# Stick-breaking scores of a Trainium2 kernel: from plain f32 matmuls to three f32r passes over split q and k

## What is computed

```python
def stick_breaking_attention(q, k, v):
    ...
    for s0, s1 in bounds:
        z = jnp.einsum('bqhd,bkhd->bhqk', q[:, s0:s1].astype(f32), k[:, :s1].astype(f32)) * scale
        strict = jnp.arange(s1)[None, :] < jnp.arange(s0, s1)[:, None]
        log_1m = jnp.where(strict, jax.nn.log_sigmoid(-z), 0.0)
        after = lax.cumsum(log_1m, axis=3, reverse=True) - log_1m
        w = jnp.where(strict, jnp.exp(jax.nn.log_sigmoid(z) + after), 0.0)
        outs.append(jnp.einsum('bhqk,bkhd->bqhd', w, v[:, :s1].astype(f32)))
```

## Time and profile before

| | us |
|---|---|
| median of 3 runs | 1746.51 (1746.11 to 1747.75) |
| span of the profiled execution | 1744.8 |
| TensorE busy in it | 1731.6 (99%) |
| VectorE busy | 1166.4 (67%) |
| ScalarE busy | 756.2 (43%) |

### The profile page before, as it was taken

One profiled execution on the slowest core, in us unless ns is written; L12 is line 12 of the kernel. 1 busy time (PEld: TensorE's weight loads), 2 busy tenths in 40 slices (PEclk: granted clock), 3 DMA queues, 4 the chain that ended last, 5 costly groups with the idle time before them and its releaser, 6 DMA issues.

```text
span 1744.8 us, 34207 instructions
## 1 busy us (share of the span) xinstructions
PE 1731.6 (99%) x13476; PEld 1653.1 (95%) x13476; DVE 1166.4 (67%) x1697; ACT 756.2 (43%) x1052; POOL 7.6 (0%) x35
## 2 busy tenths in 40 slices
PE   9999999999999999999999999999999999999998
PEld 7999999999999999999999999999989999999887
DVE  7888766556466878874334777777775688888333
ACT  5455432224334323232223877777874433233222
POOL 0000000000000000000000000000000000000000
PEclk9999999999999999999999999999999999999999
DMA  4322232222223232323223222222212322223222
GB/s 160 124 86 85 97 110 70 76 73 72 62 86 96 84 96 84 94 95 100 83 86 104 66 76 77 76 76 78 84 62 85 97 85 95 96 84 110 100 84 80
DMA packets 43887, 154.20 MB, mean 88 GB/s; under 512 B 5136, under 2 KB 8208, under 8 KB 43168
## 3 DMA queue, kind: packets, MB, share of 16 engines
q1 hardware_dynamic: 42064, 146.10, 26.7%
q10 hardware_dynamic: 1744, 6.99, 1.1%
HBM read 146.62 MB, written 2.13 MB: 85 GB/s over the span
## 4 chain that ended last, share of the span: by engine, by line
PE 94%; DVE 3%; ACT 2%; issue 1%; DMA 0%; DVEq 0%; SPq 0%; ACTq 0%
PE gp L453 81%; PE small L489 2%; PE small L654 2%; PE small L573 1%; PE small L541 1%; PE small L705 1%; PE gp L813 1%; PE small L716 1%; PE small L676 1%; PE small L481 1%; DVE wlo L1315 0%; PE small L672 0%; DVE spb L1804 0%; PE small L684 0%; ACT lbuf L1145 0%
## 5 line engine op out<-in xcount | busy, mean ns | idle before, releaser
L453 PE MATMUL gp<-hn_hi,whi 128*128 128x256 f32 (+2 forms) x3200 | 658.9, 287 | 0.4 <-DVE wlo L1315 0.2
L453 PE MATMUL gp<-hn_hi,wlo 128*128 128x256 f32 (+2 forms) x3200 | 648.0, 284 | 0.0
L453 PE MATMUL gp<-hn_lo,whi 128*128 128x256 f32 (+2 forms) x3200 | 646.7, 283 | 0.0
L843 ACT ACTIVATE whi<-raw 128x1024 fp32r<-128x1024 f32 (+1 forms) x248 | 272.9, 1101 | 720.0 <-PE gp L453 719.5
L1315 DVE TENSOR_TENSOR wlo<-raw,whi 128x1024 fp32r<-128x1024 f32 (+1 forms) x248 | 316.3, 1275 | 329.2 <-ACT whi L843 329.0
L453 PEld LDWEIGHTS gp<-hn_hi,whi 128*128 128x128 f32 x3200 | 500.6, 189 | 3.9 <-DVE wlo L1315 1.0
L453 PEld LDWEIGHTS gp<-hn_lo,whi 128*128 128x128 f32 x3200 | 498.2, 188 | 0.0
L453 PEld LDWEIGHTS gp<-hn_hi,wlo 128*128 128x128 f32 x3200 | 497.5, 188 | 0.0
L453 PE MATMUL gp<-hid_hi,wlo 128*128 128x256 f32 (+1 forms) x506 | 132.5, 318 | 0.0
L453 PE MATMUL gp<-hid_hi,whi 128*128 128x256 f32 (+1 forms) x506 | 132.4, 318 | 0.0
L453 PE MATMUL gp<-hid_lo,whi 128*128 128x256 f32 (+1 forms) x506 | 132.1, 317 | 0.0
(11 more groups left out here) (261 smaller groups left out, 1777.3 us busy)
## 6 DMA issues: line engine op xcount, KB each, us to landing
raw<-in SPq DMA_DIRECT2D x217, 512.0 KB, 3.5
raw<-in SPq DMA_DIRECT2D x32, 704.0 KB, 4.0
cs_bc<-cs_scratch ACTq DMA_DIRECT2D x4, 1056.0 KB, 5.6
q_turned<-qs SPq DMA_DIRECT2D x16, 132.0 KB, 4.3
k_turned<-ks SPq DMA_DIRECT2D x16, 132.0 KB, 4.1
hT<-in SPq DMA_DIRECT2D x3, 528.0 KB, 7.1
out<-yT SPq DMA_DIRECT2D x6, 256.0 KB, 2.4
rdec<-in ACTq DMA_DIRECT2D x1, 1056.0 KB, 7.7
```

What stands on the lines that cost most here:

```text
L453: ins = pe.matmul(psum[:, h, c0:c0 + n_cols], wp[w.par][:, cols], rp[:, k0 + k, q0:q0 + n_cols], start=first and k == 0 and n == 0, stop=l ...
L843: act.activation(whi[w.par][:, 0:kt * P], raw[w.par][:, 0:kt * P], ACT.Copy).then_inc(hi_done, 1)
```

## The change

q and k of a pair are split in a high part (f32r, a copy on ScalarE, `heads_hi`) and a low part (a subtraction on VectorE, `heads_lo`), and `scores` runs its six pieces three times: high q by high k, low q by high k, high q by low k. The split of pair n+1 stands behind the second softplus of pair n, ahead of the split of the next weights, on both engines; that of pair 0 stands in the prologue. The copies with the heads changed are now made of the split parts (12 DMAs a pair in place of 4, and of q only the columns that bank 2 needs), one weight load later in SyncE's queue, and they wait for the low parts. `qs` and `ks` have one buffer in place of two, `lbuf` is gone (the softplus works in `spb`), and the mask `never` is read from `never2`.

```diff
-                qs = [sb(f"qs{s}", [P, T], f32, s3) for s in range(2)]
-                ks = [sb(f"ks{s}", [P, T], f32, s3) for s in range(2)]
-                q_turned, k_turned = (sb(n, [P, T], f32, s3) for n in ("q_turned", "k_turned"))
+                qs, ks = (sb(n, [P, T], f32, s3) for n in ("qs", "ks"))
+                q_hi, q_lo, k_hi, k_lo = (sb(n, [P, T], f32r, s3) for n in ("q_hi", "q_lo", "k_hi", "k_lo"))
+                kt_hi, kt_lo = (sb(n, [P, T], f32r, s3) for n in ("kt_hi", "kt_lo"))
+                qt_hi, qt_lo = (sb(n, [P, N_META + T - 256], f32r, s3) for n in ("qt_hi", "qt_lo"))
...
-                lbuf = sb("lbuf", [P, CAUSAL], f32, s3)
...
             stream(W_FI0, 2 * KF, w_fi0)
             stream(W_FO0, 16, w_fo0, KH)
 
-            def turn_heads(i, b):
-
-                if isinstance(i, int) and i == 0:
-                    sp.wait_ge(zero_done, 1)
-                for c, src, dst in ((0, qs[b % 2], q_turned), (1, ks[b % 2], k_turned)):
-                    if isinstance(i, int):
-                        t = At(10, i, T_L1 + 5 * b + c)
-                        sp.wait_ge(pair_free[t.par], t.half + 1)
-                    for e in range(2):
-                        sp.dma_start(dst[HEAD * (1 - e):HEAD * (2 - e), :],
-                                     src[HEAD * e:HEAD * (e + 1), :]).then_inc(turned_in, 16)
+            def turn_heads(n):
+
+                sp.wait_ge(qklo_done, 2 * n + 2)
+                for e in range(2):
+                    to, own = slice(HEAD * (1 - e), HEAD * (2 - e)), slice(HEAD * e, HEAD * (e + 1))
+                    for src, dst in ((k_hi, kt_hi), (k_lo, kt_lo)):
+                        sp.dma_start(dst[to, :].bitcast(f32), src[own, :].bitcast(f32)).then_inc(turned_in, 16)
+                    for src, dst in ((q_hi, qt_hi), (q_lo, qt_lo)):
+                        sp.dma_start(dst[to, 0:N_META].bitcast(f32), src[own, 0:N_META].bitcast(f32)).then_inc(turned_in, 16)
+                        sp.dma_start(dst[to, N_META:].bitcast(f32), src[own, 256:T].bitcast(f32)).then_inc(turned_in, 16)
 
             def l1_pair(i):
                 for b in range(2):
...
-                        if c == 1 and not (isinstance(i, int) and b == 0):
+                        if c == 2 and not (isinstance(i, int) and b == 0):
...
-                            turn_heads(i, b - 1)
+                            turn_heads(2 * i + b - 1)
...
-            for c in range(2):
+            for c in range(3):
...
-            turn_heads(3, 1)
-            for c in range(2, KD):
+            turn_heads(7)
+            for c in range(3, KD):
...
             def scores(n, b, e, behind=None):
 
                 if e == 0:
-                    pe.wait_ge(turned_in, 64 * (n + 1))
-                for k0, q0, w, bk, c0 in SB_PIECES:
-                    if e == 1 and c0 == 0:
-                        pe.wait_ge(wb_done, 3 * n + SB_ORDER.index(bk) + 1)
-                    at = HEAD * (e if bk < 2 else 1 - e)
-                    kk, qq = (ks[b], qs[b]) if bk < 2 else (k_turned, q_turned)
-                    pe.matmul(sp_[:, bk, c0:c0 + w], kk[at:at + HEAD, k0:k0 + P],
-                              qq[at:at + HEAD, q0:q0 + w], start=c0 == 0, stop=True, skip_group_check=True)
+                    pe.wait_ge(turned_in, 192 * (n + 1))
+                own, other = slice(HEAD * e, HEAD * (e + 1)), slice(HEAD * (1 - e), HEAD * (2 - e))
+                for p, (kk, qq, kt, qt) in enumerate(((k_hi, q_hi, kt_hi, qt_hi), (k_hi, q_lo, kt_hi, qt_lo),
+                                                      (k_lo, q_hi, kt_lo, qt_hi))):
+                    for k0, q0, w, bk, c0 in SB_PIECES:
+                        first = p == 0 and c0 == 0
+                        if e == 1 and first:
+                            pe.wait_ge(wb_done, 3 * n + SB_ORDER.index(bk) + 1)
+                        if bk < 2:
+                            keys, queries = kk[own, k0:k0 + P], qq[own, q0:q0 + w]
+                        else:
+                            at = 0 if q0 == 0 else N_META + q0 - 256
+                            keys, queries = kt[other, k0:k0 + P], qt[other, at:at + w]
+                        pe.matmul(sp_[:, bk, c0:c0 + w], keys, queries, start=first, stop=p == 2,
+                                  skip_group_check=True)
                 if behind is not None:
                     behind()
-                pe.matmul(sp_[:, 0, 0:P - N_META], ident_b[:], never[:, N_META:P], start=False, stop=True,
+                pe.matmul(sp_[:, 0, 0:P - N_META], ident_b[:], never2[:, N_META:P], start=False, stop=True,
                           skip_group_check=True)
-                pe.matmul(sp_[:, 1, 0:P], ident_b[:], never[:], start=False, stop=True, skip_group_check=True)
+                pe.matmul(sp_[:, 1, 0:P], ident_b[:], never2[:, 0:P], start=False, stop=True, skip_group_check=True)
                 pe.matmul(sp_[:, 2, 0:448], ident_b[:], never2[:], start=False, stop=True,
                           skip_group_check=True).then_inc(z_done, 1)
 
...
-                    ins = act.activation(lbuf[:, at:at + w], sp_[:, b, 0:w], ACT.Abs)
+                    ins = act.activation(spb[:, at:at + w], sp_[:, b, 0:w], ACT.Abs)
...
-                ch.link(act.activation(lbuf[:], lbuf[:], ACT.Exp, scale=-1.0))
+                ch.link(act.activation(spb[:], spb[:], ACT.Exp, scale=-1.0))
...
-                    act.activation(lbuf[:, at:at + w], lbuf[:, at:at + w], ACT.Ln, bias=1.0).then_inc(l_done, 1)
+                    act.activation(spb[:, at:at + w], spb[:, at:at + w], ACT.Ln, bias=1.0).then_inc(l_done, 1)
...
             def nsp_col(n):
                 return nsp[:, bass.ds(n, 1)]
 
+            def heads_hi(i, b):
+
+                for c, (dst, src) in enumerate(((q_hi, qs), (k_hi, ks))):
+                    t = At(10, i, T_L1 + 5 * b + c)
+                    act.wait_ge(pair_free[t.par], t.half + 1)
+                    act.activation(dst[:], src[:], ACT.Copy).then_inc(qkhi_done, 1)
+
+            act.wait_ge(zero_done, 1)
             for c in range(1, 5):
                 split_hi(At(10, 0, W_L1 + c + 1))
+                if c == 3:
+                    heads_hi(0, 0)
 
             def lru_root(n):
 
...
                         turn()
 
                 soft(n, 1, last)
+                if not out:
+                    heads_hi(i, b + 1)
                 split(following)
                 lru_root(n)
 
...
-                    ve.scalar_tensor_tensor(spb[:, at:at + w], sp_[:, b, 0:w], 0.0, lbuf[:, at:at + w], ALU.max,
+                    ve.scalar_tensor_tensor(spb[:, at:at + w], sp_[:, b, 0:w], 0.0, spb[:, at:at + w], ALU.max,
...
 
                 n = 2 * i + b
                 w, t = At(10, i, W_L1 + 5 * b + c), At(10, i, T_L1 + 5 * b + c)
-                if c < 2:
-                    wait_count(ve, z_done, 2 * n - 2)
                 if c == 2:
                     wait_count(ve, tvs_done, n)
                 if c == 4:
                     wait_count(ve, xc_done, n)
-                dst = (qs[b % 2][:], ks[b % 2][:], vs, gt, ubx[:, 3:3 + T])[c]
+                dst = (qs[:], ks[:], vs, gt, ubx[:, 3:3 + T])[c]
                 t0 = FROM_MIX1 if c in (0, 3) else 0
                 evacuate(w, t, dst[:, t0:T], SB_SCALE if c == 0 else None, t0=t0)
+
+            def heads_lo(n):
+
+                for c, (dst, src, hi) in enumerate(((q_lo, qs, q_hi), (k_lo, ks, k_hi))):
+                    ve.wait_ge(qkhi_done, 2 * n + c + 1)
+                    ve.tensor_tensor(dst[:], src[:], hi[:].bitcast(f32), ALU.subtract).then_inc(qklo_done, 1)
 
             def lru_in(i, b):
 
...
                 ch.link(ve.tensor_tensor_scan(acc[:], la, lb[:], 0.0, ALU.mult, ALU.add))
                 ve.scalar_tensor_tensor(yT[:, 8 + n, :], ge, 0.5, acc[:], ALU.mult, ALU.mult).then_inc(ylru_done, 1)
 
+            ve.wait_ge(zero_done, 1)
             for c in range(4):
                 if c > 0:
                     split_lo(At(10, 0, W_L1 + c + 1))
                 l1_tile(0, 0, c)
+            heads_lo(0)
             split_lo(At(10, 0, W_L1 + 5))
 
             def l1_block(i, b, out=0, following=6, turn=None):
...
                 if turn is not None:
                     turn()
                 soft(n, 1)
+                if not out:
+                    heads_lo(n + 1)
                 split(following)
 
-            ve.wait_ge(zero_done, 1)
             for b in range(2):
                 l1_block(0, b)
             with ve.Fori(1, 3) as i:
```

More of the change, by code:

```diff
@@ L191, in build @@
         ident_b = sb("ident_b", [P, P], mybir.dt.bfloat16)
-        never = sb("never", [P, P], mybir.dt.bfloat16)
         never2 = sb("never2", [P, 448], mybir.dt.bfloat16)
@@ L342, in build @@
             sem(n) for n in ("sum_done", "sphi_done", "later_done", "lathi_done", "latlo_done"))
-        turned_in = sem("turned_in")
+        turned_in, qkhi_done, qklo_done = sem("turned_in"), sem("qkhi_done"), sem("qklo_done")
```

(4 more changed lines are left out.)

## The result

The changed kernel takes 1758.95 us (median of 4 runs, 1758.59 to 1759.33), the kernel before beside it 1747.13 (4 runs, 1746.11 to 1747.88): a ratio of 1.007, with a 95% interval of 1.0058 to 1.0083. That is +11.8 us where +3.1 was forecast: inside the range of 1745.5 to 1769.5 us, but outside the likeliest case's own, which ended at 1754. The range reached that far for the two rivals in which the scores get slower, and neither came about: that the result lies in it is luck. The span of the profiled execution went from 1744.8 to 1757.2 us, +12.4.

What follows compares the result with a forecast made beforehand. TensorE, its matmuls filling 99% of the span, was taken to bound the kernel. Scores -4.0, gates +7.1 and transfers at nothing gave +3.1 us on 1746.5, so 1749.6 us, range 1745.5 to 1769.5.

Steps and rivals of the forecast that it cites:

- likeliest case: Whole kernel: faster scores, later gates, hidden transfers; 1749.6 us, own range 1745.5 to 1754, chance 0.51.
- two rivals in which the scores get slower: Scores: halves serial, 1769.4 us, chance 0.24; or short pieces or loads cost more, 1755.8 to 1759.0 us, chance 0.16.
- The scores: TensorE's 16 score calls: 18 f32r matmuls, halves side by side, 1.47 us instead of 1.72; 4.0 us gained.
- first rival: Scores on TensorE: the halves run serially in f32r; +22.9 us, 1769.4 us, chance 0.24.
- The gates: Gate matmuls wait for VectorE's convolution, delayed 1.27 us a pair by the split, seven pairs; 7.1 us lost.
- ScalarE isn't the one that decides: Ahead of the gates: ScalarE's copies are ready before VectorE asks, weights' high part about 1122.6 against 1122.7.
- airs: Slack between convolution end and gate matmuls covering the delay: 0.61, 0.38, 0.69 us in pairs 1, 6, 7; 1.76 deducted.
- absorbed case: VectorE between softplus and conv-input evacuation: idle time and slack absorb the subtractions; 1742.5 us, chance 0.09.
- The transfers: SyncE: twelve transfers of at most 0.6 us each, and the weight load queued behind them, stay hidden; no cost.
- The sum: Whole kernel: -4.0 + 7.1 = +3.1 us on the median of 1746.5, giving 1749.6 us.
- second rival: Scores on TensorE: side by side, but a short piece or its load costs more; 1755.8 to 1759.0 us, chance 0.16.

Runs made afterwards that it cites:

- e1: Changed kernel with the output projection's fourth weight load issued ahead of the last pair's twelve transfers: 1749.4 us, ratio to before 1.0017.
- e4: Kernel before plus two unused VectorE subtractions of 128x528 at the change's place, the next split waiting for both: 1754.74 us, ratio 1.0046.
- e6: Changed kernel with the copies and subtractions of q and k on GpSimd instead of ScalarE and VectorE: 1744.06 us, ratio to before 0.9987.
- e9: e6 with only the two copies on GpSimd and the subtractions on VectorE right behind the gelu output: 1741.77 us, ratio to before 0.9974.
- e5: e1 with bank 2's pieces also reading the head's own half, so all 18 matmuls use one half: 1777.79 us, ratio to before 1.0173.
- e3: e1 with VectorE's two subtractions of pairs 1 to 7 cut from 528 to 16 columns: 1747.75 us, ratio to before 1.0007.
- e8: e3 with ScalarE's two copies of pairs 1 to 7 also cut to 16 columns: 1742.81 us, ratio to before 0.998.
- e7: Kernel before with the output projection's fourth weight load held until the last pair's gate products are done: 1753.81 us against 1746.31, ratio 1.0042.

## Why the prediction was right in two terms and wrong in the third

**The scores: -4.0 forecast, -3.6 measured** (e1 less before in the second and third column: -1.55 and -2.03). Some 0.4 us of the second column belong to the gates, as e4 shows; in e6 and e9, where the gates wait no more than before, the same two columns stand 4.0 below it, as forecast. The call is 1.47 to 1.48 us, where 1.47 was forecast. The two paces that the sum was made of, 0.11 us for a short matmul and 1/2.4 ns a column, hold in the halves too. The first rival falls by the timeline, and e5 prices it.

**The gates: +7.1 forecast, +6.6 measured.** With the 0.4 us that they put into the second column it is 7.0. All seven waits came at the place named, 0.33 to 1.16 us, 5.5 us together, where 0.6 to 1.6 and 7 together were announced: the profile's idle time is less than the delay, since the rows of consecutive matmuls overlap. The prediction's "ScalarE isn't the one that decides" holds by 0.22 us in pair 4, but it suggests more than it should: with VectorE's part taken away only 1.2 us came back (e3), with both parts 6.0 (e8). A chain that leads by 0.2 us is worth 0.2 us a pair to remove. To ask which of two engines decides was the wrong question; the answer for a repair is the distance to the second.

**Small slips in its sums.** The airs that the prediction names for pairs 1, 6 and 7 add up to 1.68 us, and the 0.08 up to the 1.76 that it takes off aren't worked out (they may be what its 0.13 to 0.17 us leave at pairs 2, 3 and 5); with 1.68 its sum is 7.2. The low end of the likeliest case by its own terms is 1746.5 - 6.2 + 5.9 = 1746.2 and not 1745.5. Its bound for the absorbed case doesn't quite come out either: 7 x 0.33 - 1.76 is 0.55 and not under 0.5. None of this changes the forecast.

**The transfers: 0 forecast, +9.5 measured. This step failed**, in the words: "Queued behind them on SyncE is the next weight load: ... the split that reads it is the fourth on ScalarE from there, behind the gates and the next scores; hidden." For pairs 1 to 6 the place is right, behind the gates and the next scores, though the count isn't: in pair 4 the load goes at 1131.56, and its split is the next one on ScalarE, at 1142.98. In these six pairs the load landed 5.4 to 7.7 us ahead of its split. The issue cost (0.60 us, short ones too) was nearly right, 0.64 us from one start to the next, and SyncE was free at 1131.2 in pair 4 where 1130.0 was forecast. But I read it in a middle pair and put it down for all. In the last pair no further head pair's projections follow: the load behind the transfers is the output projection's fourth unit, and its split stands ahead of the gates' tanh and not behind it. Even before, that load landed only 7.2 us ahead of its split (1256.11 to 1263.30), where pair 4's landed 14.8 us ahead. e1 takes away that order alone and the 9.5 us with it, e7 makes the delay alone and gets 8.2. What is queued behind the moved transfers was looked at in one kind of pair out of two.

**Its size** had a second part that no row before could show. 5.4 us of waiting cost 9.5, because the clock then stayed at 0.50 for 10.24 us: the call of the scores in it took 2.70 us.

**The sum.** With the load in time (e1), the median is +3.2 over before, the forecast +3.1. So the mechanism of the forecast held but for one load of 512 KB in one pair of eight. The 1758.95 us lie where the second rival had its times, 1755.8 to 1759.0, but for another reason than that rival's: no call of the scores got slower but the one that ran at the lower clock.

## What to carry to other kernels

A transfer's issue time occupies its queue: price what is queued behind it at the first, a middle and the last iteration, since the hand-written order at a loop's end is another program. Where two engines feed a wait side by side, find how far apart they are before naming one; the cheaper repair is often to move the work to where the engine waits anyway (e9). And a TensorE wait of some us has to be priced with the clock that follows it.

## What the hardware showed

- After 5.4 us without a matmul (4.3 in e7) TensorE was at the 1.2 GHz level for 10.24 us; the clock fell 4.2 us after the last matmul (2.6 in e7), within the wait. The waits of up to 1.2 us at the gates were never followed by that.
- In e5, with the matmuls of 64 rows in one half only, the clock was at 0.50 in six stretches of 3.4 us, each right behind a call of the scores of a first head, though TensorE hadn't waited for 7.9 us or more. With both halves in use (e1) this never came.
- A transfer of 4 KB costs SyncE's queue as much to issue as one of 132 KB (medians of 0.60 us, and 0.57 and 0.60), and a weight load 0.33. The 4 KB land after 1.9 us (median), the 132 KB after 2.3.
- f32r matmuls of 64 rows in different halves run side by side: a call takes 1.48 us with that, 2.83 without.
- VectorE's split of 128x1024 took 1.45 us beside GpSimd's subtractions (1.44 to 1.60 in pairs 1 to 7) and 1.22 without; GpSimd's own took 1.3 to 1.9 us for 128x528, where VectorE's takes 0.70.
